# The last slab with tokens as the stationary operand, its token tiles ending one by one

## The reference

```python
h = h + sq_relu_mlp(rmsnorm(h, norm_ffn[layer]), ffn_w_up[layer], ffn_w_down[layer])
...
def sq_relu_mlp(u, w_up, w_down):
    a = jax.nn.relu(u @ w_up)
    return (a * a) @ w_down
...
def rmsnorm(x, g):
    y = x * lax.rsqrt(jnp.mean(x * x, axis=-1, keepdims=True) + EPS)
    return y * g
...
return (rmsnorm(h, norm_final), ...)
```

## Time and profile before

| | |
|---|---|
| time, median of 3 runs | 2503.55 us (2501.21 to 2508.31) |
| profiled execution, its time | 2500.25 us |
| its span, first to last instruction | 2498.5 us |
| PE busy | 2468.6 us (99%) |
| DVE, ACT, POOL busy | 1210.0, 903.2, 490.1 us |
| mean granted TensorE clock, as a share of full speed | 0.994 |

### The profile page before, as it was taken

The page is one execution under the profiler, slowest core; times in us unless marked ns, Lnnn a source line. Parts: engine busy times, 40 slices in busy tenths (PEclk is TensorE's granted clock), DMA queues, the critical chain, the costliest instruction groups (busy, mean ns, idle before and its releaser), DMA issues.

```text
span 2498.5 us, 43768 instructions
## 1 busy us (share of the span) xinstructions
PE 2468.6 (99%) x16527; PEld 2423.9 (97%) x16527; DVE 1210.0 (48%) x1391; ACT 903.2 (36%) x1053; POOL 490.1 (20%) x620
## 2 busy tenths in 40 slices
PE   9999999999999999999999999999999999999998
PEld 8999999999999999999888889999999999999997
DVE  6644444444444454454478885544444444444443
ACT  4333233333333333333355553333233333323332
POOL 6430022012102232210011122230022012102221
PEclk9999999999999999999999999999999999999999
DMA  6554454444444554555376664544454445444442
GB/s 188 152 151 147 149 150 151 147 148 150 151 146 148 151 151 129 150 147 158 105 237 216 228 194 151 151 150 148 149 151 149 147 149 151 149 147 148 141 150 91
DMA packets 197126, 385.03 MB, mean 154 GB/s; under 512 B 12053, under 2 KB 12165, under 8 KB 196645
## 3 DMA queue, kind: packets, MB, share of 16 engines
q1 hardware_dynamic: 196780, 383.88, 50.3%
q0 software_dynamic: 272, 0.14, 0.0%
HBM read 361.78 MB, written 22.64 MB: 154 GB/s over the span
## 4 chain that ended last, share of the span: by engine, by line
PE 95%; DVE 3%; DMA 1%; ACT 1%; issue 0%; SPq 0%; ACTq 0%
PE G L1527 30%; PE G L1529 30%; PE G L1528 30%; PE X L1789 1%; PE X L1752 1%; DVE w_lo L1076 0%; DMA w_raw<-in_mlstm_w_out 0%; PE X L1796 0%; DMA gain<-in_norm_mix 0%; DVE qkv L1343 0%; PE X L1512 0%; DVE cst L1450 0%; PE X L1513 0%; PE X L1741 0%; PE X L1731 0%
## 5 line engine op out<-in xcount | busy, mean ns | idle before, releaser
L1076 DVE TENSOR_TENSOR w_lo<-w_raw,w_hi 128x1024 fp32r<-128x1024 f32 x648 | 828.7, 1281 | 1174.7 <-ACT w_hi L779 1170.6
L779 ACT ACTIVATE w_hi<-w_raw 128x1024 fp32r<-128x1024 f32 x608 | 642.7, 1058 | 1315.3 <-PE G L1529 1296.1
L1527 PE MATMUL G<-op_hi,w_hi 128*128 128x320 f32 x2816 | 874.9, 311 | 2.2 <-DVE w_lo L1076 1.5
L1528 PE MATMUL G<-op_lo,w_hi 128*128 128x320 f32 x2816 | 869.4, 309 | 0.0
L1529 PE MATMUL G<-op_hi,w_lo 128*128 128x320 f32 x2816 | 869.3, 309 | 0.0
L1527 PE MATMUL G<-a_hi,w_hi 128*128 128x320 f32 x2368 | 730.7, 309 | 2.7 <-DVE a_lo L1355 2.1
L1529 PE MATMUL G<-a_hi,w_lo 128*128 128x320 f32 x2368 | 729.8, 308 | 0.0
L1528 PE MATMUL G<-a_lo,w_hi 128*128 128x320 f32 x2368 | 729.8, 308 | 0.0
L1527 PEld LDWEIGHTS G<-op_hi,w_hi 128*128 128x128 f32 x2816 | 530.0, 188 | 10.4 <-issue 6.1
L1528 PEld LDWEIGHTS G<-op_lo,w_hi 128*128 128x128 f32 x2816 | 530.1, 188 | 2.6 <-issue 1.0
L1529 PEld LDWEIGHTS G<-op_hi,w_lo 128*128 128x128 f32 x2816 | 530.0, 188 | 0.0
(11 more groups left out here) (269 smaller groups left out, 974.0 us busy)
## 6 DMA issues: line engine op xcount, KB each, us to landing
w_raw<-in_ffn_w_up SPq DMA_DIRECT2D x256, 512.0 KB, 3.7
w_raw<-in_ffn_w_down SPq DMA_DIRECT2D x256, 512.0 KB, 3.9
w_raw<-in_mlstm_w_in SPq DMA_DIRECT2D x96, 512.0 KB, 3.9
w_raw<-in_mlstm_w_out SPq DMA_DIRECT2D x32, 512.0 KB, 4.3
cst<-in_state_mlstm_C SPq DMA_DIRECT2D x24, 512.0 KB, 4.3
out_C_sample<-cst SPq DMA_DIRECT2D x24, 512.0 KB, 3.2
w_raw<-in_pool_w SPq DMA_DIRECT2D x8, 512.0 KB, 10.9
w_raw<-in_state_mlstm_C SPq DMA_DIRECT2D x8, 512.0 KB, 4.1
```

The costliest lines, as they stand in the source:

```text
L779: act.activation(w_hi[:, c % RING], w_raw[:, c % RING], ACT.Copy).then_inc(w_hi_ok, 1)
L1076: v.tensor_tensor(w_lo[:, slot], w_raw[:, slot], w_hi[:, slot].bitcast(F32), ALU.subtract).then_inc(w_lo_ok, 1)
L1527: pe.matmul(G[:, m, 0:T], w_hi[:, slot, t, w], hi[:, k, :], start=first and t == 0, stop=False)
L1528: pe.matmul(G[:, m, 0:T], w_hi[:, slot, t, w], lo[:, k, :], start=False, stop=False)
```

## The change

Only the last slab (`S_END - 1`, output features 1536 to 2047) and what follows it are rewritten.

- The operands are exchanged: for each k-tile the stationary operand is 128 tokens of `a_hi` or `a_lo`, the moving one the 512 weight columns, and the result lies token-major in `G[:, t]`, t = 0, 1, 2. Tiles 0 and 1 take three matmuls a k-tile. The 64 sample tokens take two: ACT writes a stationary tile `s_pair` of 64 columns of `a_hi` beside 64 of `a_lo` ahead of time (`sample_pairs`, two instructions, in the slab `S_END - 3`, into `op_lo`, which is free by then), and the two halves of the bank are added at the end. That makes 16 x 8 = 128 matmuls of 512 columns.
- The first four chunks go chunk by chunk over all three tiles. The last four are run tile by tile in the order 2, 0, 1 (`LAST_TILES`), since the four slots hold them all; so the tiles end one by one.
- The residual of these features is added by 12 float32 matmuls of `hT` against the identity into the same banks, after the third chunk. `token_sums(acc)` (three products) stands after the fourth.
- `y_back`, `keep` and the transposes are gone. Per tile: ACT squares the bank with a running sum over the 512 features (for tile 2 after the halves are joined), DVE adds the sum of the other features, takes the reciprocal, ACT the root; DVE writes the last 512 features of `yrow` from the bank with the root and the gain in one instruction. PE spreads the root of each token over the partitions (`widen`, one float32 matmul into `X[t]`), and DVE multiplies the first 12 tiles of `yT` by it, feature-major.
- `widen(n - 1)` stands in PE's stream ahead of the last chunk of the next tile; the last one stands behind everything.
- Features 0 to 1535 are stored feature-major (`y_first`), the last 512 token-major (`y_last`); the host puts them into their places. SP also loads the last 512 gains onto all partitions (`fin_gain`). There are six stores as before, now of 128, 384, 256, 768, 256 and 768 KB; before there were four of 512 KB and two of 256 KB.

The core of the diff:

```diff
+FT = KT - MT
+LAST_TILES = (2, 0, 1)
@@ SP
+            sp.dma_start(fin_gain, A["norm_final"]...[:, D - NC:].broadcast_to([P, NC])).then_inc(fin_in, 16)
+            for n, t in enumerate(LAST_TILES):
+                rows = tok(t)
+                sp.wait_ge(y_done, 2 * n + 1)
+                sp.dma_start(O["y_last"][rows, :], yrow[0:ROWS[t], t, D - NC:]).then_inc(y_out, 16)
+                sp.wait_ge(y_done, 2 * n + 2)
+                sp.dma_start(O["y_first"][:, FT * rows.start:FT * rows.stop], yrow[:, t, 0:FT * ROWS[t]]).then_inc(y_out, 16)
@@ ACT
+                act.wait_ge(last_done, n + 1)
+                if t == 2:
+                    act.activation(s_half, G[NS:P, t, :], ACT.Copy).then_inc(half_ok, 1)
+                    act.wait_ge(both_ok, 1)
+                act.activation(relu[rows, 0:2, :]..., s_half if t == 2 else G[rows, t, :],
+                               ACT.Square, accum_out=scol[rows, t:t + 1]).then_inc(sq_end, 1)
+                act.wait_ge(tail_inv, n + 1)
+                act.activation(r, r, ACT.Sqrt).then_inc(tail_r, 1)
@@ DVE
+                link(v.scalar_tensor_tensor(out=r, in0=scol[rows, t:t + 1], scalar=1.0 / D, in1=xcol[rows, t:t + 1],
+                                            op0=ALU.mult, op1=ALU.add))
+                v.reciprocal(r, r).then_inc(tail_inv, 1)
+                v.wait_ge(tail_r, n + 1)
+                v.scalar_tensor_tensor(out=yrow[rows, t, D - NC:], in0=s_half if t == 2 else G[rows, t, :], scalar=r,
+                                       in1=fin_gain[rows, :], op0=ALU.mult, op1=ALU.mult).then_inc(y_done, 1)
+                v.wait_ge(r_wide, n + 1)
+                v.tensor_tensor(yrow[:, t, 0:FT * ROWS[t]]..., yT[:, 0:FT, tok(t)],
+                                bc(X[t][:, 0:ROWS[t]], [P, FT, ROWS[t]]), ALU.mult).then_inc(y_done, 1)
@@ PE
-                     (lambda c: y_back(j - 1) if c == 1 else None) if j else None)
+            for c in range(CH - RING):
+                pe.wait_ge(w_lo_ok, chunk_no(s, c) + 1)
+                for t in range(TT):
...
+                    ins = tokens(t, c)
+                ins.then_inc(gemm, 1)
+                if c == 2:
+                    for t in range(TT):
+                        for m in range(MT):
+                            pe.matmul(G[0:ROWS[t], t, m * P:(m + 1) * P], hT[:, KT - MT + m, tok(t)], ident[:, :],
+                                      start=False, stop=False, skip_group_check=True)
             pe.wait_ge(ssq_ok, 4 * KT - MT)
-            token_sums(acc, True, False)
-            for m in range(MT):
-                pe.wait_ge(sq_end, m + 1)
-                ins = token_sums(relu[:, m], False, m == MT - 1)
-            ins.then_inc(r_sum, 1)
-            y_back(MT - 1)
+            token_sums(acc, True, True).then_inc(sums_ok, 1)
+            for n, t in enumerate(LAST_TILES):
+                for c in range(CH - RING, CH):
+                    if n == 0:
+                        pe.wait_ge(w_lo_ok, chunk_no(s, c) + 1)
+                    if n and c == CH - 1:
+                        widen(n - 1)
+                    ins = tokens(t, c, c == CH - 1)
+                ins.then_inc(last_done, 1)
+            widen(TT - 1)
```

More of the change, by code:

```diff
@@ L1052, in _, with sample_pairs @@
-            act.wait_ge(a_lo_ok, 2 * SLICES * KT)
-            for j in range(MT):
-                slab(S_END - MT + j, end_square if j == MT - 1 else None, {2: lambda: keep(j - 1)} if j else None,
-                     last=j == MT - 1)
-            keep(MT - 1)
-            root(4, rcol[:, 0:TT], rcol[:, 0:TT])
-            act.wait_ge(r_ok, 4)
-            act.wait_ge(y_kept_a, 2 * MT)
-            act.wait_ge(y_kept_d, MT)
-            for t, half in ACT_HALVES:
-                y = yrow[0:ROWS[t], t, half * D // 2:(half + 1) * D // 2]
-                act.activation(y, y, ACT.Copy, scale=rcol[0:ROWS[t], t:t + 1]).then_inc(y_done_a, 1)
+            def sample_pairs():
+                act.wait_ge(gemm, tile_done(S_END - MT - 1, MT - 1))
+                for n, part in enumerate((a_hi, a_lo)):
+                    act.activation(s_pair[:, :, n * NS:(n + 1) * NS], part[:, :, TP:T].bitcast(F32), ACT.Copy).then_inc(pair_ok, 1)
@@ L1479, in _ @@
             ffn(1, S_FFN1, 3)
[L1480 to L1485 removed]
+            for j in range(MT - 1):
                 def evict(m, j=j):
@@ L1498, in _ @@
-            keep(MT - 1)
-            v.wait_ge(r_ok, 4)
-            v.wait_ge(y_kept_a, 2 * MT)
-            v.wait_ge(y_kept_d, MT)
-            for t, half in DVE_HALVES:
-                y = yrow[0:ROWS[t], t, half * D // 2:(half + 1) * D // 2]
-                v.tensor_scalar(y, y, rcol[0:ROWS[t], t:t + 1], None, ALU.mult).then_inc(y_done_d, 1)
+                slab(S_END - MT + j, evict)
+            for c in range(LEAD, CH):
+                split(S_END - 1, c)
+            v.wait_ge(sums_ok, 1)
@@ L1842, with results @@
          ("m_sample", (1, NSEQ, HEADS))]
+def results(out):
+    y = np.empty((T, D), np.float32)
+    first = np.asarray(out["out_y_first"])
+    for at, n in ((0, P), (P, P), (TP, NS)):
+        y[at:at + n, 0:D - NC] = first[:, FT * at:FT * (at + n)].reshape(P, FT, n).transpose(2, 1, 0).reshape(n, D - NC)
+    y[:, D - NC:] = out["out_y_last"]
+    return (y[0:TP].reshape(1, TP, D), y[TP:].reshape(NSEQ, TS, D), *(out[f"out_{name}"] for name, _ in _OUTS[2:]))
 def kernel(**inputs):
@@ L1858 @@
     r = run_bass_kernel_spmd(nc, [arrays], core_ids=[0])
[L1859 removed]
+    return results(r.results[0])
```

109 lines of the change are left out of this document (66 added, 43 removed).

## The result

The changed kernel takes 2487.99 us (median of 14 runs, 2483.84 to 2496.89), the kernel before 2503.7 in the runs beside it (14 runs, 2496.85 to 2512.07). The ratio is 0.9937, with a 95% interval of 0.9924 to 0.9949: 15.7 us less. The profiled execution took 2488.81 with a span of 2487.1, against 2500.25 and 2498.5 before: 11.4 less, where 10.6 was forecast.

A forecast was written before the change was run, and what follows sets the result against it. The kernel was taken as one stream of PE matmuls with a start and a tail. The stream gains nothing, the tail falls from 19.24 to 8.5 us: 10.6 less, 2489.7 profiled, 2493.0 median, range 2489.5 to 2499.0.

The forecast's parts named there:

- The turns: PE's stream: three turns (`y_turn`, with transposes) taken out at 2.09 us each, 6.3 us less.
- The slab: Last slab: 128 matmuls of 512 columns at 0.232 us, 29.7 us against 28.15 before, so 1.5 us more.
- The rival of cheap columns: Last slab: 512-column matmuls at about 131 ns, as the skill page has it, slab 16.8 us, kernel 2480.1; chance 1%.
- The residual, the sums, the two `widen`: Work added to PE's stream in the last slab: 3.2, 0.8 and 0.9 us.
- B: Time at which PE is free of the last slab: forecast 2479.4, bounds 2478.1 to 2481.0; 2479.26 before.
- The covers: Last slab: PE work hides other engines' waits; 1.0 us left at the last chunk's split, root of tile 2 3.0 against 4.2.
- The rival of waits between the tiles: Last slab: late split or root chain leaves PE standing; 2 us at both places take back 4, giving 2497.0; chance 12%.
- The tail up to the last store: Behind B: square done at 0.9 us, root 1.6, gain product 2.3, widened product 4.1, last store issued 4.15.
- The landing: End of kernel: the last store, 768 KB, lands 3.9 us after issue, between 3.2 (all latency) and 4.8 (all bytes).
- From the profiled time to the median: Whole kernel: median taken to stand 3.3 us above the profiled execution, so 2489.7 gives 2493.0.
- The falling clock: Last slab: one-column sums drop the clock to 1.2 GHz, 64 matmuls cost 14 us more, giving 2507; chance 4%.
- Tiles ending together: Last slab: if tiles end together, tile 0's store and product stand behind B, 3.7 us more, 2496.7; chance 2%.

The follow-up runs named there:

- the pair with the scatter removed: Kernel before and changed kernel, both with extra identity matmuls filling PE's idle places in the first 22 us: 2500.35 and 2486.2 us.
- two ways: Kernel before with filled start, plus either the unused tile `scol` (2499.9 us) or output tensors of the changed kernel's sizes (2500.72 us).

## Why the prediction was right or wrong

**The turns** (6.3). Right: put back, they cost 2.09 in the last slab and 4.2 ahead of it.

**The slab** (29.7 at 0.232). Right: 34.25 less residual, sums and two `widen` leaves 29.7, and the neighbours stand 0.23 apart. The rival of cheap columns is out, by these 0.23 us in fp32r. The Trainium skill, "TensorE: Matmul & The Clock Gate", Back-to-back issue gap, gives about 131 ns for this width in a stream of load and matmul pairs. The trace does not agree with it.

**The residual, the sums, the two `widen`** (3.2, 0.8, 0.9). 3.0, 0.75 and 0.8, each within its bounds. Their errors are all of one sign and add up to 0.35. That B came at 2479.33 where 2479.4 was said is in part luck: from S to B it took 34.25 where 34.55 follows from the terms, and S came 0.27 later than the removed turns put it. The range of B, 2478.1 to 2481.0, was far too wide for terms read from near rows.

**The covers.** Right: no matmul of the last slab has an idle time before it. `w_lo` of the last chunk is ready 0.9 ahead of PE, where 1.0 was said (DVE's row at 2464.29 and 1.23, against 2463.58 and twelve times 0.232); the root of tile 2 is done 1.3 ahead of `widen(0)`, where 1.2 was said. The rival of waits between the tiles did not come.

**The tail up to the last store** (B + 0.9, 1.6, 2.3, 4.1, 4.15). Right: B + 0.9, 1.6, 2.3, 4.0 and 4.07. DVE's product of 1536 elements took 1.74, where 1.7 to 1.8 came out of forms of 512 and 1024.

**The landing** (3.9). Mis-sized: about 3.2 for 768 KB, and from issue to the end of the span 3.7 instead of 4.35. I had put the larger store between "all latency" (3.2) and "all bytes" (4.8), both reckoned from 512 KB in 3.2. The bytes do count: 256 KB landed after 2.0, 384 after 2.3, 768 after 3.2. What was too high is the starting point. The stores of that row are of the mLSTM part, where a load of weights is issued 0.4 us behind one of them (1412.28 and 1412.70 in the trace of the kernel before); whether that load is what slows them was not tested. This term is 0.65 of the miss of 5.0, and it was in the stated range.

**The clock behind B.** A term that was not in the sum as such. The price of the old tail was read from one execution, in which the clock fell to the 1.2 GHz level 3 us behind B. In five executions the tail of that kernel lies between 18.8 and 20.25, 19.5 on average: 0.3 us more than in the one read. The change removes that spread with the work.

**From the profiled time to the median** (3.3 taken as constant). This is the step that failed: it makes 4.1 of the miss of 5.0, while the forecast of the profiled execution, 2489.7, missed its 2488.81 by 0.9, most of it the landing. The offset is no property of the kernel: it is where this execution fell among runs that scatter by 13 to 15 us. For the changed kernel it was -0.8, with 14 runs beside it. Pooled over the first 40 runs of the kernel before and 21 of the changed one the difference of means is 14.4, give or take 2.2, and in the pair with the scatter removed it is 14.15. So of the 15.7 about 1.5 is the draw, 12.1 the steps by the trace, and about 2, give or take 1, are left over. The traces put some 1.7 of them in the mLSTM part, which the forecast had held to be untouched. How the change reaches there is not known; two ways were tried, and one trace of each speaks against them.

**The rivals.** Stores, waits, cheap columns: out, as above. The falling clock: the mechanism exists (the run with ten times the sums), but three products do not set it off, and after sixty its price was 2 us for the matmuls behind them, not 14. Tiles ending together: 3.1 us more when it was made so, where 3.7 was said.

## What to carry to other kernels

Sum a change against the distances between two landmarks of the trace (here the last slab's start and PE's last matmul), and treat the distance from a profiled execution to the median as an unknown of the size of the runs' scatter, not as a constant. If runs of a kernel scatter by ten times what its stages do, look at the granted clock in its first 50 us, and fill PE's idle stretches there before measuring anything that is worth less. And when PE's stream neither gains nor loses, the gain of a reordering lies in what leaves the tail: compute that can end tile by tile should, with the smallest last store that its issue time allows.

## What the runs showed of the hardware

- ACT's splits in the mLSTM part, which wait for loads of 512 KB, come sooner in the changed kernel though no instruction there differs: after 12.9 to 13.2 us and 16.2 to 17.0 (ten traces) against 13.2 to 13.4 and 16.9 to 18.9 (five), counted from the last head's state products.
- A PE that is busy with one-column products all the time still loses the clock: granted 0.78 and then 0.50 within a row of 60 records, which took 9.84 us in place of the 6.3 that ten times 0.63 would be.
- Filling PE's idle stretches at the start takes the scatter of runs from 15 us to 3, and costs nothing (2500.35 against 2500.87 beside it). An idle stretch brings a fall of the clock in some executions and not in others.
- At the end of the changed kernel a store of 256 KB lands after 2.0 us, one of 384 KB after 2.3 and one of 768 KB after 3.2; a last store of half the size ends the span 0.8 sooner.
- Part of the mLSTM stretch's time is a draw of the clock: 1.7, 3.4 or 5.1 us lost in each of 17 traces.
